# Eleven of fourteen projections of x made of three rounded fp32r products each

## The reference

```
h = rms_norm(x, norm_mix_g)
proj = h @ w_in                    # 1024 -> 2304 columns
q_sb, k_sb, v_sb, x_rg, gate_rg, q_ca = split(proj, 512, 512, 512, 256, 256, 256)
o_sb = stick_breaking_attention(q_sb, k_sb, v_sb)      # 8 heads of 64
xc   = causal_depthwise_conv(x_rg)                     # width 4
o_rg = gelu(gate_rg) * rg_lru(xc)
o_ca = memory_cross_attention(q_ca, mem, w_mem_kv)     # 4 heads, 256 memory tokens
x = x + concat(rms_norm of the three) @ w_out
x = x + moe(rms_norm(x))                               # 64 experts, top 8, and a shared one
```

## Time and profile before

| what | us |
|---|---|
| median of three runs | 597.85 |
| the profiled execution | 599.13 |
| span of its trace | 597.4 |
| TensorE busy in the span | 562.9 |
| VectorE / ScalarE busy | 196.8 / 147.9 |
| DMA, mean over the span | 381 GB/s |

### The profile page before, as it was taken

One profiled execution on the slowest core, in us unless ns is written; L12 is line 12 of the kernel. 1 busy time (PEld: TensorE's weight loads), 2 busy tenths in 40 slices (PEclk: granted clock), 3 DMA queues, 4 the chain that ended last, 5 costly groups with the idle time before them and its releaser, 6 DMA issues.

```text
span 597.4 us, 8118 instructions
## 1 busy us (share of the span) xinstructions
PE 562.9 (94%) x3060; PEld 307.5 (51%) x3061; DVE 196.8 (33%) x522; ACT 147.9 (25%) x296; POOL 20.3 (3%) x78
## 2 busy tenths in 40 slices
PE   8999998999999999999999999999998999589984
PEld 6888774456454444445445444554444455145321
DVE  2347687756322522222122222222222022121112
ACT  5273246425211111110011111111111111111102
POOL 1012131000000000000000000000000000000000
PEclk9999999999999999999999999999999899798988
DMA  8996359808999999999999999999999999999993
GB/s 316 419 423 259 140 215 366 354 21 355 417 411 399 425 421 419 422 431 418 431 425 426 424 427 422 421 426 426 429 421 423 430 423 428 421 426 425 423 400 123
DMA packets 28072, 227.49 MB, mean 381 GB/s; under 512 B 3328, under 2 KB 3456, under 8 KB 7808
## 3 DMA queue, kind: packets, MB, share of 16 engines
q1 hardware_dynamic: 27888, 226.93, 91.7%
q10 hardware_dynamic: 144, 0.03, 0.0%
HBM read 225.90 MB, written 1.05 MB: 380 GB/s over the span
## 4 chain that ended last, share of the span: by engine, by line
PE 73%; DMA 15%; SPq 4%; ACT 3%; DVE 2%; issue 1%; DVEq 0%; ACTq 0%
PE ps L1668 27%; PE ps L1697 11%; DMA cell_two<-in_w_gu_e 10%; PE ps L1634 8%; PE ps L1419 7%; PE ps L1707 6%; DMA cell_gu<-in_w_gu_e 5%; PE ps L1541 4%; SPq L398 4%; PE ps L1436 4%; PE ps L1688 1%; PE ps L1426 1%; DMA wA<-in_w_qk 1%; PE ps L1674 1%; PE ps L1680 1%
## 5 line engine op out<-in xcount | busy, mean ns | idle before, releaser
L1668 PE MATMUL ps<-cell_two,xg 128*64 128x512 f32 (+2 forms) x640 | 125.4, 618 | 13.9 <-DMA cell_two<-in_w_gu_e 13.9
L1697 PE MATMUL ps<-cell_d,e_hT 128*64 128x512 f32 (+2 forms) x512 | 95.2, 597 | 1.9 <-DVE e_hT L1304 1.5
L1668 PEld LDWEIGHTS ps<-cell_two,xg 128*64 128x64 f32 (+2 forms) x640 | 40.8, 133 | 96.8 <-issue 96.8
L1668 PE MATMUL ps<-cell_gu,xg 128*64 128x512 f32 (+2 forms) x416 | 79.5, 608 | 2.7 <-DMA cell_gu<-in_w_gu_e 2.7
L1301 DVE TENSOR_TENSOR e_h<-e_sg,ps 128x256 f32<-128x256 f32 x28 | 11.8, 421 | 185.5 <-ACT e_sg L819 185.5
L819 ACT ACTIVATE e_sg<-ps 128x256 f32<-128x256 f32 x28 | 10.7, 384 | 214.7 <-PE ps L1668 214.7
L1363 DVE SCALAR_TENSOR_TENSOR ylo<-ps,gslot,yhi 128x512 fp32r<-128x512 f32 x52 | 39.1, 751 | 72.8 <-ACT yhi L833 72.8
L1634 PE MATMUL ps<-pick,xhi 128*128 128x256 f32 x224 | 58.5, 300 | 0.3 <-DVE pick L1217 0.3
L1634 PE MATMUL ps<-pick,xlo 128*128 128x256 f32 x224 | 54.3, 281 | 0.0
L833 ACT ACTIVATE yhi<-ps,gslot 128x512 fp32r<-128x512 f32 x52 | 35.7, 687 | 70.0 <-PE ps L1697 70.0
L1668 PEld LDWEIGHTS ps<-cell_gu,xg 128*64 128x64 f32 (+2 forms) x416 | 25.5, 131 | 52.8 <-issue 52.6
(11 more groups left out here) (315 smaller groups left out, 515.7 us busy)
## 6 DMA issues: line engine op xcount, KB each, us to landing
cell_two<-in_w_gu_e SPq DMA_DIRECT2D x40, 2048.0 KB, 26.9
cell_d<-in_w_down_e SPq DMA_DIRECT2D x60, 1024.0 KB, 27.1
cell_gu<-in_w_gu_e SPq DMA_DIRECT2D x48, 1024.0 KB, 18.5
wo<-in_w_out SPq DMA_DIRECT2D x1, 4096.0 KB, 13.6
wA<-in_w_qk SPq DMA_DIRECT2D x7, 512.0 KB, 11.0
wR<-in_w_rest SPq DMA_DIRECT2D x3, 1024.0 KB, 28.5
wV<-in_w_v SPq DMA_DIRECT2D x1, 2048.0 KB, 19.0
w_kv<-in_w_mem SPq DMA_DIRECT2D x1, 2048.0 KB, 26.8
```

The lines of the kernel that those rows point to most:

```text
L1668: last = mm(ps[side * w:(side + 1) * w, U, :], rows(k, slice(side * w, (side + 1) * w)), weight[:, k - k0, :], start=k == 0, stop=k == KD - 1)
L1697: last = mm(ps[side * w:(side + 1) * w, Y[half], :], e_hT[:, kk, side * w:(side + 1) * w], cell_d[n][:, kk, half * 512:(half + 1) * 512], ...
```

## The change

Units 3 to 7, 10, 11 and 14 to 17 go over to three products a step, with hT_hi and hT_lo and high and low parts of their weights. Units 0, 1 and 2 stay plain fp32. A new `split_u` (n) rounds unit n's weights on ScalarE into a buffer of 4 KB a partition (8 KB for the one of units 10 and 11) and makes the low part on VectorE in the place of the weights. The splits stand in `walk`, and ScalarE and VectorE do them there. hT and hT_lo change places in SBUF. The waits shown above stay, but the counts of `whi_act` and `wlo_dve` are taken from the place of a split in `walk`.

```diff
+    hi_at = [r.offset - 4 * KB, r.offset, o_ring + 56 * KB, o_ring + 60 * KB, o_ring + 88 * KB]
+    hi_unit = [at(f"hi_unit{i}", offset, [P, KD, P], F32R) for i, offset in enumerate(hi_at)]
+    hi_wR2 = at("hi_wR2", o_ring + 88 * KB, [P, KD, 256], F32R)
...
-        walk = [("unit", 0), ("unit", 1), ("unit", 2), ("row", 0), ("unit", 3), ("unit", 4), ("split_w", 0), ("unit", 5),
-                ("split_w", 1), ("unit", 6), ("mem_norm", 0), ("unit", 7), ("split_a", 1)]
+        walk = [("split_u", 3), ("split_u", 4), ("unit", 0), ("unit", 1), ("unit", 2), ("row", 0), ("split_u", 5), ("unit", 3),
+                ("split_u", 6), ("unit", 4), ("split_u", 7), ("split_w", 0), ("unit", 5),
+                ("split_w", 1), ("unit", 6), ("mem_norm", 0), ("unit", 7), ("split_u", 10), ("split_a", 1)]
...
-            walk += {2: [("split_w", 2)], 3: [("split_w", 3)], 5: [("log1p", 0)], 7: [("ca_square", 0)], 8: [("ca_norm", 0)], 9: [("conv", 0)],
+            walk += {1: [("split_u", 14)], 2: [("split_w", 2)], 3: [("split_w", 3)], 4: [("split_u", 15)], 5: [("log1p", 0)],
+                     6: [("split_u", 16), ("split_u", 17)], 7: [("ca_square", 0)], 8: [("ca_norm", 0)], 9: [("conv", 0)],
...
+        hi_place = {3: 0, 4: 1, 5: 2, 6: 3, 7: 0, 14: 2, 15: 3, 16: 0, 17: 4}
+        hi_left = {7: 3, 14: 5, 15: 6, 16: 7, 17: 11}
...
+            def split_u(n):                                  # ScalarE
+                if n < 8:
+                    act.wait_ge(wA_loaded[n], 16)
+                else:
+                    act.wait_ge(wR_loaded[2 if n == 10 else rg_cols[n][0]], 16)
+                if n in hi_left:
+                    act.wait_ge(unit_ps, hi_left[n] + 1)
+                w, hi, lo = split_of(n)
+                nc.scalar.copy(hi, w).then_inc(whi_act, 1)
...
+            def split_u(n):                                  # VectorE
+                dve.wait_ge(whi_act, split_count("split_u", n))
+                w, hi, lo = split_of(n)
+                nc.vector.tensor_tensor(lo, w, hi.bitcast(F32), ALU.subtract).then_inc(wlo_dve, 1)
...
+                if ("split_u", n) in splits and n != 10:     # TensorE
+                    pe.wait_ge(wlo_dve, split_count("split_u", n))
+                    pe.wait_ge(alo_dve, 1)
+                    w, w_hi, w_lo = split_of(n)
+                    for k in range(KD):
+                        for m, (a, part) in enumerate(((hT_hi, w_hi), (hT_lo, w_hi), (hT_hi, w_lo))):
+                            last = mm(b[:, 0:SEQ], part[:, k, :], a[:, k, :], start=k == 0 and m == 0, stop=k == KD - 1 and m == 2)
...
-                            last = mm(b[:, 0:CA], hT[:, k, c:c + P], wR[2][:, k, :], start=k == 0, stop=k == KD - 1)
+                            for m, (a, w) in enumerate(((hT_hi, hi_wR2), (hT_lo, hi_wR2), (hT_hi, wR_lo[2]))):
+                                last = mm(b[:, 0:CA], a[:, k, c:c + P], w[:, k, :], start=k == 0 and m == 0,
+                                          stop=k == KD - 1 and m == 2)
```

More of the change, by code:

```diff
@@ L143, in hybrid_decoder_layer @@
     x_in = at("x_in", o_ring + 56 * KB, [P, NT, D])
-    hT = at("hT", o_ring + 48 * KB, [P, KD, SEQ])
+    hT = at("hT", o_ring + 24 * KB, [P, KD, SEQ])
     hT_hi = at("hT_hi", o_ring + 16 * KB, [P, KD, SEQ], F32R)
-    hT_lo = at("hT_lo", o_ring + 24 * KB, [P, KD, SEQ], F32R)
+    hT_lo = at("hT_lo", o_ring + 48 * KB, [P, KD, SEQ], F32R)
     wV_hi = at("wV_hi", o_ring + 32 * KB, [P, KD, 512], F32R)
@@ L158, in hybrid_decoder_layer @@
     wA = [at(f"wA{n}", o_A + 4 * KB * n, [P, KD, P]) for n in range(8)]
+    wA_lo = [at(f"wA_lo{n}", o_A + 4 * KB * n, [P, KD, P], F32R) for n in range(8)]
     wo = at("wo", o_A, [P, KD, D])
@@ L170, in hybrid_decoder_layer @@
     wR = [at(f"wR{g}", o_R + 8 * KB * g, [P, KD, 256]) for g in range(3)]
+    wR_lo = [at(f"wR_lo{g}", o_R + 8 * KB * g, [P, KD, 256], F32R) for g in range(3)]
     r = Space(o_R)
@@ L338, in hybrid_decoder_layer, with split_count, split_of @@
                 walk.append(("t", i - 3))
-            walk += {2: [("split_w", 2)], 3: [("split_w", 3)], 5: [("log1p", 0)], 7: [("ca_square", 0)], 8: [("ca_norm", 0)], 9: [("conv", 0)],
+            walk += {1: [("split_u", 14)], 2: [("split_w", 2)], 3: [("split_w", 3)], 4: [("split_u", 15)], 5: [("log1p", 0)],
+                     6: [("split_u", 16), ("split_u", 17)], 7: [("ca_square", 0)], 8: [("ca_norm", 0)], 9: [("conv", 0)],
                      11: [("gelu", 0)]}.get(i, [])
         rg_cols = {14: (0, 0), 15: (0, P), 16: (1, 0), 17: (1, P)}
+        hi_place = {3: 0, 4: 1, 5: 2, 6: 3, 7: 0, 14: 2, 15: 3, 16: 0, 17: 4}
+        hi_left = {7: 3, 14: 5, 15: 6, 16: 7, 17: 11}
+        splits = [item for item in walk if item[0] in ("split_u", "split_w")]
+        def split_count(kind, n):
+            return splits.index((kind, n)) + 1
+        def split_of(n):
+            if n < 8:
+                return wA[n][:], hi_unit[hi_place[n]][:], wA_lo[n][:]
+            if n == 10:
+                return wR[2][:], hi_wR2[:], wR_lo[2][:]
+            g, c = rg_cols[n]
+            return wR[g][:, :, c:c + P], hi_unit[hi_place[n]][:], wR_lo[g][:, :, c:c + P]
         SUMS = (26, 33, 34)
@@ L693, in split_w @@
                 nc.scalar.copy((wV_hi, w_kv_hi)[i // 2][:, c, :], (wV, w_kv)[i // 2][:, c, :]).then_inc(whi_act, 1)
+            def split_u(n):
+                if n < 8:
+                    act.wait_ge(wA_loaded[n], 16)
[5 more added lines that the diff above has]
+                nc.scalar.copy(hi, w).then_inc(whi_act, 1)
             split_a(0)
@@ L711, in _ @@
                     split_w(n)
+                elif kind == "split_u":
+                    split_u(n)
                 elif kind == "mem_norm":
@@ L952, in split_w @@
             def split_w(i):
-                dve.wait_ge(whi_act, i + 1)
+                dve.wait_ge(whi_act, split_count("split_w", i))
                 c = slice(i % 2 * 4, i % 2 * 4 + 4)
@@ L1400, in unit @@
                 b = ps[:, n % 4, :]
[L1401 to L1410, removed]
+                if ("split_u", n) in splits and n != 10:
[5 more added lines that the diff above has]
+                            last = mm(b[:, 0:SEQ], part[:, k, :], a[:, k, :], start=k == 0 and m == 0, stop=k == KD - 1 and m == 2)
+                elif n < 8:
+                    if n:
+                        pe.wait_ge(wA_loaded[n], 16)
+                    w, c = wA[n], 0
                     for k in range(KD):
@@ L1422, in unit @@
                     if n in (10, 11):
-                        pe.wait_ge(wR_loaded[2], 16)
+                        pe.wait_ge(wlo_dve, split_count("split_u", 10))
                         c = (n - 10) * P
                         for k in range(KD):
-                            last = mm(b[:, 0:CA], hT[:, k, c:c + P], wR[2][:, k, :], start=k == 0, stop=k == KD - 1)
+                            for m, (a, w) in enumerate(((hT_hi, hi_wR2), (hT_lo, hi_wR2), (hT_hi, wR_lo[2]))):
+                                last = mm(b[:, 0:CA], a[:, k, c:c + P], w[:, k, :], start=k == 0 and m == 0,
+                                          stop=k == KD - 1 and m == 2)
                     else:
@@ L1433, in unit @@
                             if k % 4 == 0:
-                                pe.wait_ge(wlo_dve, 2 * i + k // 4 + 1)
+                                pe.wait_ge(wlo_dve, split_count("split_w", 2 * i + k // 4))
                             for m, (a, w) in enumerate(((a_hi, w_hi), (a_lo, w_hi), (a_hi, w_lo))):
```

## The result

The changed kernel is slower: 602.73 us, median of six runs (601.65 to 604.11), against 597.62 us (596.91 to 600.12) of the kernel before in six runs on the same chip. The ratio is 1.0071, 95% interval 1.0052 to 1.0091, that is +4.2 us (3.1 to 5.4) on 597.6; the two medians by themselves lie 5.1 us apart. The forecast was +3.0 us and 600.8 us; the sign and the mechanism hold, two terms of the sum were too small. The profiled execution took 601.99 us, its span is 600.2 us.

What follows compares the result with a forecast made beforehand. The early stages bound the kernel by setting when the weight stream restarts: 2.05 (z 0) + 1.5 (clock) - 1.26 (units 10, 11) + 0.3 (unit 12) + 0.38 (splits 16, 17) = +3.0 us, median 600.8 us, range 599.0 to 602.6.

Steps and rivals of the forecast that it cites:

- one for one: Last stage, the DMA stream of weights: any shift of its restart moves the end by the same amount.
- TensorE's saving: Each converted unit on TensorE: 2.92 us instead of 3.55, 0.63 us less.
- Splits 3 to 7: Early stretch where ScalarE and VectorE wait for work: these splits cost nothing, TensorE gains 3.1 us.
- Split 10 ahead of the memory's split: Before z 0: memT_lo ends at 42.4 us, z 0 2.05 us late, TensorE's gap about 5 us.
- The clock: After the gap at z 0: granted clock falls to half, costing 1.5 us in unit 9, bounds 0 to 1.9.
- Unit 12's wait and z 4: Unit 12 waits 0.3 us for the second half of w_kv_lo; z 4 comes 2.6 us late.
- Splits 16 and 17: VectorE's closed stretch from z 4: 2.3 us of work, idle time swallows 1.92, convolution another 0.38 us late.
- A: Gap at z 0: clock stays up or returns before costing anything; +1.5 us, 599.35 us; chance 0.2.
- B: At unit 20: VectorE has slack and is not last, TensorE's account decides; 596.1 to 597.6 us; chance 0.1.
- C: Converted units: three products run as long as a plain unit; +2.6 us, 600.4 us; chance 0.1.
- D: ScalarE and VectorE: extra work delays more than seen (splits 14, 15 or w_kv); +5 us, 602.9 us; chance 0.15.
- 14 and 15: Splits in VectorE's idle times: cost nothing; 1.15 us each if that cover were gone.

Runs made afterwards that it cites:

- z0_wait_on_act: Changed kernel with z 0's wait for all of memT_lo moved from TensorE to ScalarE's sigmoid of z 0; 599.86 us, ratio 1.0006 to the kernel before.
- only_3_to_7: Changed kernel with only units 3 to 7 as three products, the six others plain fp32 without splits, hT and hT_lo back in place; 596.94 us, ratio 0.9961.
- split10_after_mem: Changed kernel with split 10 moved behind the memory's split in walk; 598.55 us, ratio 0.9997 to the kernel before.
- late_splits_early: Changed kernel with splits 16 and 17 moved right behind split 15, into VectorE's idle time ahead of z 4; 600.45 us, ratio 1.0048.
- clock_filled: Changed kernel with eleven plain matmuls of zeros added ahead of z 0's wait to fill TensorE's gap; 601.39 us, ratio 1.0056.
- both_moved: Changed kernel with split 10 behind the memory's split and splits 16 and 17 behind split 15; 596.76 us, ratio 0.9973.
- both_moved_filled: Changed kernel with split 10 and splits 16 and 17 moved, plus five plain matmuls ahead of unit 20's wait for the convolution; 595.81 us, ratio 0.9938.
- both_moved_act_wait: Changed kernel with split 10 and splits 16 and 17 moved, and z 0's wait for memT_lo put on ScalarE; 596.99 us, ratio 0.9968.

## Why the prediction was right or wrong

**What bounds the kernel; one for one.** Right. The restart of the stream is 4.50 us late, like the gather; the measured ratio gives +4.2 us. The two spans differ by less (2.8 us), though from unit 20 on every mark up to the restart differs by 4.5 or 4.6. The ten traces show how far one for one holds: from the gather to the end of the span they take 453.6 us (the changed kernel) to 455.7 us (z0_wait_on_act), 455.4 in the kernel before. So it holds to about 1 us either way in single executions. The profiled execution of before also lay 1.5 us over its median of six, that of the changed kernel 0.7 us under its own. Why the last stage differs by up to 2 us from trace to trace stays open.

**TensorE's saving.** Right: a unit of three products took 2.96 us beside other work where 2.92 was forecast from the gather's row. The Trainium skill ("TensorE: Matmul & The Clock Gate", Back-to-back issue gap) would have given 2.73 us by an estimate from its 262 cycles; the measurement speaks for the row.

**Splits 3 to 7 for nothing.** Right; only_3_to_7 shows it alone.

**Split 10 ahead of the memory's split.** Right: z 0 late by 1.86 us (2.05 forecast), the gap 4.86 (about 5). split10_after_mem takes it back.

**The clock.** The mechanism was right, its term mis-sized: 1.5 us forecast, 2.57 us measured by filling the gap, over the upper bound of 1.9. The bounds came from falls at whose end the clock was back 2.5 to 3.7 us after work resumed; here it took 5.6 us. The nearest case of before, 7.45 us, had the fall inside the gap as well, and I should have left the upper end open.

**Unit 12's wait and z 4.** z 4 was late by 3.73 us: 1.86 + 2.58 at unit 10 (4.44 in all), less 1.17 for the two units, plus 0.46 that unit 12 took longer by (6.10 us from its start to z 4 instead of 5.64), where a wait of 0.3 was forecast. Forecast 2.6 in all, nearly all of the difference being the clock's.

**Splits 16 and 17.** Mis-sized: 0.38 us forecast, 93.97 - 89.33 - 3.73 = 0.91 measured. I let the idle time of 1.92 us ahead of z 6 swallow them, but that idle time ends with GpSimd's mask, and the subtraction itself stretched the mask from 0.54 to 1.92 us. late_splits_early shows both; there the two splits are worth 1.41 us, of which the saving of the units ahead of z 6 hid 0.6 us here (the mask starts at 79.11 us, where 75.97 in the kernel before and z 4's 3.73 would give 79.70). The sum as measured up to conv is 1.86 + 2.58 - 1.17 + 0.46 + 0.91 = 4.64 us, against +3.0.

**Rivals.** A (clock stays up) is refuted by the windows; clock_filled, which makes A, was still at 1.0056, so without the fall the change would have been slower too. B (VectorE has slack at unit 20) is refuted: a gap of 2.38 us there. C is refuted by 2.96 us. D is not borne out: 14 and 15 were covered, and w_kv_lo cost 0.46 us where 0.3 was forecast. The median, 602.73 us, lies nearer to D's 602.9 than to the forecast's 600.8, and just above the end of the range; that is no sign for D, as the excess came from the clock and from the mask. By the ratio, 4.2 us on 597.85, the time is 602.1.

## What to carry to other kernels

A cheaper form of matmul that needs preparing on other engines is priced by where the preparing stands in their order, not by its sum: here one item placed ahead of another cost 4 us at the gather, and the same work one place later left a time that can't be told from the kernel before; a gain came only with both moves, or with fewer units. A wait that opens on TensorE can cost twice, itself and the half clock behind it, so count each new gap with the slow stretch that may follow (here gaps from 1.68 us on had one, not every time); a handful of idle matmuls ahead of the wait is a cheap cure (both_moved_filled). And look at what else reads memory beside added VectorE work on two operands from SBUF: GpSimd's mask took more than three times as long.

## What the runs showed of the hardware

That GpSimd slows beside VectorE's subtraction of two SBUF operands, 1.92 us for two masks instead of 0.54, was already to be seen in the trace of before (a pair of masks took 1.54 us at 56.63 us, beside the subtraction of w_kv_lo, and 1.15 us at 79.41 us; most of the others took 0.54) and I had read over it. The Trainium skill ("GPSIMD Engine Reference", the table of its specifications) says that GpSimd's SBUF interfaces are shared with VectorE and contended by instructions with two SBUF inputs; the trace agrees, by the same 1.92 against 0.54 us.

The clock fell with waits of TensorE of 1.68 us (z0_wait_on_act), 1.95 us (both_moved_act_wait) and 2.38 us (five of seven), and not with those of 1.16 to 1.45 us ahead of z 0 (four profiles). With the waits of 1.68 and 1.95 us, and in clock_filled and both_moved, it fell only 0.9 to 1.5 us after TensorE had taken up work again; in the three other profiles it fell inside the wait of 2.38 us. A wait of the same length gave a fall in one execution and none in another, so the profile of one execution can hold a microsecond that the next does not.
